# Two transformer blocks on one core: column sums for two norms, token sums for three, modulation sums in parts, and down units by tile

## The reference

```
mod = silu(c) @ ada_w + ada_b                 # six vectors of 2048: shift, scale, gate, twice
h = modulate(rms_norm(x), shift_a, scale_a)   # norm x0
proj = h @ w_in                               # latents q (512), kv (256), rope key, 8 heads of differential q, k, v
q = rms_norm(q_lat) @ w_uq ; kv = rms_norm(kv_lat) @ w_ukv      # norms q and kv
y = concat(mla attention, rms_norm(differential attention)) @ w_o
x = x + gate_a * rms_norm(y)                  # norm y1
h = modulate(rms_norm(x), shift_f, scale_f)   # norm x1
y = (gelu(conv(h @ w_up)_gate) * conv(h @ w_up)_value) @ w_down
x = x + gate_f * rms_norm(y)                  # norm y2
```

## Time and profile before

| | |
|---|---|
| median of three runs | 1850.67 us |
| profiled execution | 1848.06 us, its span 1846.0 us |
| mean granted TensorE clock | 0.966 of full speed |
| PE busy | 1760.6 us (95% of the span) |
| DVE busy | 1245.1 us (67%) |
| ACT busy | 905.2 us (49%) |
| POOL busy | 103.0 us (6%) |
| moved by DMA | 377.15 MB, mean 204 GB/s |

### The profile page before, as it was taken

One profiled execution on the slowest core, in us unless ns is written; L12 is line 12 of the kernel. 1 busy time (PEld: TensorE's weight loads), 2 busy tenths in 40 slices (PEclk: granted clock), 3 DMA queues, 4 the chain that ended last, 5 costly groups with the idle time before them and its releaser, 6 DMA issues.

```text
span 1846.0 us, 33909 instructions
## 1 busy us (share of the span) xinstructions
PE 1760.6 (95%) x14140; PEld 1717.7 (93%) x14140; DVE 1245.1 (67%) x1784; ACT 905.2 (49%) x1490; POOL 103.0 (6%) x61
## 2 busy tenths in 40 slices
PE   4799999999999999999999999999799999999997
PEld 3799889999999999999999999999799999998897
DVE  7996899696667667667667656655564565655653
ACT  8454445454555445445445445434544654555543
POOL 0002331123200000000000000000000000000000
PEclk9899999899979999999999999999799999999998
DMA  9798788587817656656666655544145433653331
GB/s 377 300 406 301 243 269 289 188 284 265 307 55 245 222 195 229 218 197 229 216 201 227 217 187 183 183 161 160 58 161 175 145 126 134 232 196 117 110 116 46
DMA packets 103255, 377.15 MB, mean 204 GB/s; under 512 B 11584, under 2 KB 11968, under 8 KB 102976
## 3 DMA queue, kind: packets, MB, share of 16 engines
q1 hardware_dynamic: 103104, 374.99, 58.6%
HBM read 372.85 MB, written 2.10 MB: 203 GB/s over the span
## 4 chain that ended last, share of the span: by engine, by line
PE 86%; DVE 8%; issue 3%; DMA 1%; ACT 1%; DVEq 0%; SPq 0%; ACTq 0%
PE ps L580 25%; PE ps L581 24%; PE ps L582 24%; DVE ada_acc L1495 3%; PE ps L689 2%; PE ps L631 2%; PE ps L611 1%; DMA raw<-in_ada 1%; PE ps L723 1%; PE ps L708 1%; PE ps L731 1%; DVE w_lo L1480 1%; DVE probs L1626 1%; PE ps L673 1%; DVE stats L1600 1%
## 5 line engine op out<-in xcount | busy, mean ns | idle before, releaser
L580 PE MATMUL ps<-h_hi,w_hi 128*128 128x256 f32 x3264 | 946.1, 290 | 12.1 <-DVE h_lo L1562 6.2
L581 PE MATMUL ps<-h_lo,w_hi 128*128 128x256 f32 x3264 | 929.6, 285 | 0.0
L582 PE MATMUL ps<-h_hi,w_lo 128*128 128x256 f32 x3264 | 929.1, 285 | 0.0
L1480 DVE TENSOR_TENSOR w_lo<-raw,w_hi 128x1024 fp32r<-128x1024 f32 x481 | 587.9, 1224 | 312.7 <-ACT w_hi L1084 310.0
L1084 ACT ACTIVATE w_hi<-raw 128x1024 fp32r<-128x1024 f32 x512 | 539.8, 1056 | 427.9 <-PE ps L582 402.0
L580 PEld LDWEIGHTS ps<-h_hi,w_hi 128*128 128x128 f32 x3264 | 632.4, 194 | 18.2 <-issue 15.1
L581 PEld LDWEIGHTS ps<-h_lo,w_hi 128*128 128x128 f32 x3264 | 632.6, 194 | 1.1
L582 PEld LDWEIGHTS ps<-h_hi,w_lo 128*128 128x128 f32 x3264 | 632.3, 194 | 0.0
L1495 DVE SCALAR_TENSOR_TENSOR ada_acc<-raw,c_act,ada_acc 128x1024 f32<-128x1024 f32 x180 | 236.0, 1323 | 4.4 <-DMA raw<-in_ada 0.8
L580 PE MATMUL ps<-g_hi,w_hi 128*128 128x256 f32 x704 | 199.4, 283 | 3.7 <-DVE g_lo L1862 3.7
L582 PE MATMUL ps<-g_hi,w_lo 128*128 128x256 f32 x704 | 198.6, 282 | 0.0
(11 more groups left out here) (220 smaller groups left out, 1347.0 us busy)
## 6 DMA issues: line engine op xcount, KB each, us to landing
raw<-in_weights SPq DMA_DIRECT2D x512, 512.0 KB, 4.2
raw<-in_ada SPq DMA_DIRECT2D x192, 512.0 KB, 4.9
x<-in_x SPq DMA_DIRECT2D x1, 2048.0 KB, 13.9
out_y<-x SPq DMA_DIRECT2D x3, 512.0 KB, 2.8
consts<-in_consts SPq DMA_DIRECT2D x1, 798.0 KB, 7.9
out_y<-x SPq DMA_DIRECT2D x2, 256.0 KB, 3.1
params<-in_params SPq DMA_DIRECT2D x1, 504.0 KB, 6.4
probs<-in_pos_q SPq DMA_DIRECT2D x1, 128.0 KB, 2.0
```

What stands on the lines that cost most here:

```text
L580: nc.tensor.matmul(out, wh, hi[:, k, :], start=start, stop=False)
L581: nc.tensor.matmul(out, wh, lo[:, k, :], start=False, stop=False)
L582: last = nc.tensor.matmul(out, wl, hi[:, k, :], start=False, stop=stop)
L1480: V.tensor_tensor(w_lo[:, h % W_SLOTS, :], raw[:, raw_slot("w", h), :], w_hi[:, h % W_SLOTS, :].bitcast(F32), ALU.subtract).then_inc(lo_dv ...
```

## The change

- The sums of x1 and x2 go by `mean_square` (256 moving columns). ACT's root reads the sums in PSUM and does the division and epsilon itself; DVE inverts 256 columns; there is no widening, and `modulate` reads `rstd` in SBUF.
- The sums of x0, q and kv go by `token_sums`; their root and inverse have two columns, and a widening puts them in PSUM, from where the scales read them. kv's scale moves from unit 12 to unit 10.
- Sum 4 is issued in four parts behind steps 2 to 5, sum 5 in four parts behind units 11 to 14 of w_o's first pass, sum 6 in four parts behind units 11 to 14 of its second pass, sum 7 in eight parts behind the last eight down units of the fifth group. The waits stand before the first part. `PLAN` brings the ada blocks of sum 6 forward, from one behind each of 15 units to 15 behind the first 11.
- In the last feed-forward group the first four down units run tile by tile, each tile as it is ready.
- A root of one column (`root_table`) is taken by ACT ahead of the loops for y1, y2 and x3, outputs that nothing reads. For y1 the low part of one half moves from before the mean to between mean and inverse.

```diff
@@ -168,3 +168,3 @@
         + [2, 2, 2, 1, 2, 2, 2, 1, 2, 2, 1, 1, 1, 2, 1, 1]
-        + [1] * 15 + [0])
+        + [2, 1, 2, 1, 2, 1, 1, 1, 2, 1, 1] + [0] * 5)
 PLAN_FIRST = [64 + sum(PLAN[:n]) for n in range(len(PLAN) + 1)]
...
@@ -518,5 +519,9 @@
         SCALED = dict(y1=0, y2=len(CHUNKS))
-        TOKEN = dict(y1=0, x1=1, y2=2, x2=3, x3=4)
-        WIDE_BANK = dict(y1=5, x1=3, y2=2, x2=3, x3=2)
+        TOKEN = dict(x0=0, q=1, kv=2, y1=3, y2=4, x3=5)
+        TOKEN_TILES = dict(x0=KT, q=4, kv=2, y1=KT, y2=KT, x3=KT)
+        TOKEN_COLUMN = dict(x0=0, q=0, kv=8, y1=0, y2=0, x3=0)
+        WIDE_BANK = dict(x0=7, q=6, kv=6, y1=5, y2=2, x3=2)
+        WIDE_COLUMN = dict(x0=0, q=0, kv=S, y1=0, y2=0, x3=0)
         NORM = dict(x0=0, q=1, kv=2, y1=3, x1=4, y2=5, x2=6, x3=7)
+        FEATURES = dict(x0=D, q=512, kv=256, y1=D, y2=D, x3=D)
         HN = dict(x0=0, x1=16, x2=32)
...
@@ -603,12 +608,15 @@
-            def mod_sum(n):
+            def mod_sum(n, part=0, parts=1):
                 v, first, end = SUMS[n]
-                pe.wait_ge(ada_used, 1 + max(ADA_AT[v, b, KT - 1] for b in range(first // SLAB, end // SLAB)))
-                if n >= 2:
-                    pe.wait_ge(mod_ready, n - 1)
-                for f in range(first, end):
+                if part == 0:
+                    pe.wait_ge(ada_used, 1 + max(ADA_AT[v, b, KT - 1] for b in range(first // SLAB, end // SLAB)))
+                    if n >= 2:
+                        pe.wait_ge(mod_ready, n - 1)
+                size = (end - first) // parts
+                for f in range(first + size * part, first + size * part + size):
                     last = nc.tensor.matmul(ps[:, SCORE + n % 2, f:f + 1], ada_acc[:, v % 2, f * P:f * P + P],
                                             mean_mat[:, 0:1], start=True, stop=True)
-                last.then_inc(mod_summed, 1)
+                if part == parts - 1:
+                    last.then_inc(mod_summed, 1)
...
@@ -797,5 +806,7 @@
             pe.wait_ge(bias_ready, 6)
-            mean_square("x0", KT)
+            for k in range(KT):
+                token_sums("x0", k)
             mod_sum(0)
             pe.wait_ge(bias_ready, 8)
+            widen("x0")
             mod_sum(1)
@@ -817,7 +828,12 @@
                 if j == 6:
-                    mean_square("q", 4)
+                    for k in range(4):
+                        token_sums("q", k)
                 elif j == 8:
-                    mean_square("kv", 2)
+                    pe.wait_ge(mean_ready, TOKEN["q"] + 1)
+                    for k in range(2):
+                        token_sums("kv", k)
+                    widen("q")
+                elif j == 10:
+                    widen("kv")
                 elif j == 9:
-                    pe.wait_ge(mean_ready, NORM["q"] + 1)
                     pe.wait_ge(unit_evac, U_IN_B + KR + 1)
@@ -847,5 +863,7 @@
                     diff(14 + g)
-                elif g == 5:
+                if g == 2:
                     pe.wait_ge(exps_done, M_MLA)
-                    mod_sum(4)
+                if g in (2, 3, 4, 5):
+                    mod_sum(4, g - 2, 4)
+                if g == 5:
                     sub_sums()
@@ -873,5 +891,6 @@
                     step(m_maps, j - 1)
-                if j == 13:
+                if j == 11:
                     pe.wait_ge(exps_done, M_B)
-                    mod_sum(5)
+                if 11 <= j < 15:
+                    mod_sum(5, j - 11, 4)
             for j in range(KT):
@@ -880,8 +899,7 @@
                     token_sums("y1", j - 1)
+                if 11 <= j < 15:
+                    mod_sum(6, j - 11, 4)
             token_sums("y1", KT - 1)
             widen("y1")
-            mod_sum(6)
-            for k in range(KT):
-                token_sums("x1", k)
-            widen("x1")
+            mean_square("x1", KT)
@@ -911,8 +929,17 @@
                     unit(u + j, range(FF_GROUP), g_hi, g_lo)
-            mod_sum(7)
+                    if g == FF_FULL - 1 and j >= 8:
+                        mod_sum(7, j - 8, 8)
             for j in range(2 * FF_LAST):
                 unit(U_FFL + j, range(KT), h_hi, h_lo)
-            pe.wait_ge(g_lo_done, FF_TILES)
+            u = U_FFL + 2 * FF_LAST
+            for t in range(FF_LAST):
+                pe.wait_ge(g_lo_done, FF_GROUP * FF_FULL + t + 1)
+                for j in range(4):
+                    if t == 0:
+                        bank_free(u + j)
+                        pe.wait_ge(*lo_done(half_of(u + j)))
+                    product(UNIT_FIRST[u + j] + t, ps[:, BANK[u + j], 0:S], t, g_hi, g_lo, t == 0, t == FF_LAST - 1)
             for j in range(KT):
-                unit(U_FFL + 2 * FF_LAST + j, range(FF_LAST), g_hi, g_lo)
+                if j >= 4:
+                    unit(u + j, range(FF_LAST), g_hi, g_lo)
                 if j >= 4:
@@ -922,5 +949,3 @@
             widen("y2")
-            for k in range(KT):
-                token_sums("x2", k)
-            widen("x2")
+            mean_square("x2", KT)
             pe.wait_ge(consts_cast, 2)
@@ -1103,9 +1128,15 @@
                 n = NORM[stage]
-                act.wait_ge(mean_ready, n + 1)
-                nc.scalar.activation(rstd[:, n % 2, :], rstd[:, n % 2, :], ACT.Sqrt).then_inc(root_ready, 1)
+                act.wait_ge(sq_used, SQ[stage] + KT)
+                nc.scalar.activation(rstd[:, n % 2, :], ps[:, NORM_BANK[stage], 0:S], ACT.Sqrt, bias=eps_col[:, 0:1],
+                                     scale=1.0 / D).then_inc(root_ready, 1)
             def token_root(stage):
-                act.wait_ge(mean_ready, NORM[stage] + 1)
+                act.wait_ge(mean_ready, TOKEN[stage] + 1)
                 r = token_r[:, TOKEN[stage], :]
-                nc.scalar.activation(r, r, ACT.Sqrt, bias=eps_col[:, 0:1], scale=1.0 / D).then_inc(root_ready, 1)
+                nc.scalar.activation(r, r, ACT.Sqrt, bias=eps_col[:, 0:1], scale=1.0 / FEATURES[stage]
+                                     ).then_inc(root_ready, 1)
+
+            def root_table():
+
+                nc.scalar.activation(table_out[:, :], eps_col[:, :], ACT.Sqrt)
@@ -1218,3 +1249,3 @@
             hi(1)
-            root("x0")
+            token_root("x0")
             act.wait_ge(mod_ready, 2)
@@ -1245,5 +1276,5 @@
                     squares("kv", 2, lambda k: proj1[:, KVLAT + k, :], (unit_evac, lambda k: U_IN_B + KVLAT + k + 1))
-                    root("q")
+                    token_root("q")
                 elif j == 9:
-                    root("kv")
+                    token_root("kv")
                 elif j == 14:
@@ -1297,2 +1328,3 @@
                     step1(m_maps, j - 1, take_mla)
+            root_table()
             for j in range(KT):
@@ -1308,3 +1340,3 @@
             squares("x1", KT, lambda k: x[:, k, :], (x_ready, lambda k: XN["y1"] + k + 1))
-            token_root("x1")
+            root("x1")
             act.wait_ge(mod_ready, N_SUMS[SH_F])
@@ -1357,3 +1390,3 @@
             squares("x2", KT, lambda k: x[:, k, :], (x_ready, lambda k: XN["y2"] + k + 1))
-            token_root("x2")
+            root("x2")
             h_high("x2")
@@ -1513,9 +1547,2 @@
-            def mean(stage, tiles, n_features):
-
-                n = NORM[stage]
-                dve.wait_ge(sq_used, SQ[stage] + tiles)
-                V.tensor_scalar(rstd[:, n % 2, :], ps[:, NORM_BANK[stage], 0:S], 1.0 / n_features, EPS, ALU.mult,
-                                ALU.add).then_inc(mean_ready, 1)
-
             def invert(stage):
@@ -1527,6 +1554,10 @@
-                dve.wait_ge(sq_used, SQ[stage] + KT)
+                at, tiles = TOKEN_COLUMN[stage], TOKEN_TILES[stage]
+                dve.wait_ge(sq_used, SQ[stage] + tiles)
                 V.reduce_sum(token_r[:, TOKEN[stage], :],
-                             ps[:, NORM_BANK[stage], 0:2 * KT].rearrange("p (a k) -> p a k", a=2), AX
+                             ps[:, NORM_BANK[stage], at:at + 2 * tiles].rearrange("p (a k) -> p a k", a=2), AX
                              ).then_inc(mean_ready, 1)
+
+            def token_invert(stage):
+
                 dve.wait_ge(root_ready, NORM[stage] + 1)
...
@@ -1725,3 +1756,3 @@
                 if i == 29:
-                    mean("x0", KT, D)
+                    token_mean("x0")
                     dve.wait_ge(lam_exp, 1)
@@ -1731,3 +1762,3 @@
                     mod_out(0)
-            invert("x0")
+                    token_invert("x0")
             modulate("x0", lambda k: scale_cols[:, 0, k:k + 1], SH_A, 0, SLAB, 4, 1)
@@ -1749,3 +1780,3 @@
                         V.scalar_tensor_tensor(out=normal_in(HN["x0"] + k), in0=x[:, k, :],
-                                               scalar=scale_cols[:, 0, k:k + 1], in1=rstd[:, NORM["x0"] % 2, :],
+                                               scalar=scale_cols[:, 0, k:k + 1], in1=wide("x0"),
```

(31 more changed lines are left out.)

16 lines of the change are left out of this document (9 added, 7 removed).

## The result

| | before | after |
|---|---|---|
| median | 1851.22 us (4 runs, 1847.46 to 1852.44) | 1832.82 us (4 runs, 1831.11 to 1832.85) |
| profiled execution, its span | 1848.06, 1846.0 us | 1832.85, 1831.0 us |
| mean granted TensorE clock | 0.966 | 0.983 |
| DVE on ada blocks (180 of them) | 236.0 us | 246.2 us |

The ratio after to before is 0.9902, 95% interval 0.9885 to 0.9919: the changed kernel is 18.4 us faster by the medians and 15.2 by the two profiled executions. The forecast was 1827 in a range of 1816 to 1838. The sum of the prediction was -22.3, so some 4 us are missing by the medians and 7 by the profiles, where before's own execution was 3 us quicker than its median.

A forecast was written before the change was run, and what follows sets the result against it. PE, holding 86% of the last-ending chain, was taken to bound the kernel, its clock mattering most. Terms sum to -22.3 from 1848.06, giving 1825.8 us; with the median 2.6 above the profiled run, it forecast 1827, range 1816 to 1838.

The forecast's parts named there:

- the forecast's own case: Whole kernel: 1819 to 1833 us from the bounds of the latent norms, sum 4 and the clock's warm-up; chance 0.69.
- x1, -6.1: Norm x1: without sum 6 ahead, wide sums warm the clock and end 6.5 us earlier, chain behind +0.4; -6.1 us.
- x2, -3.8: Norm x2: wide sums end 4.2 us earlier, with no modulation sum in front, chain behind +0.4; -3.8 us.
- The rival of sums at 1.2 GHz throughout: x1 and x2: the wide sums stay at 1.2 GHz, price 4.2 us in each, 1835 us; chance 0.12.
- q and kv, -5.1: Latent norms: shorter DVE queue cuts PE's wait before the turned values, -3.0 us; scores avoid half clock, -2.1 us.
- Sum 4, -3.0: Subln sums: with sum 4 in parts ahead, they run some 3 us at full pace and end 3.0 us earlier.
- Sum 5, -1.7; sum 7, -1.7: Behind these modulation sums: issued in parts, the clock holds instead of 3.4 us at half rate; 1.7 us saved each.
- down units, -4.0: Last feed-forward group: first four down units, run tile by tile, end 4.8 us earlier, y2 sum waits 0.7; -4.0 us.
- Sum 6 inside w_o, +3.0: w_o's second pass: sum 6's parts cost PE 3.5 us less 0.5 of waiting; DVE has room for ada blocks; +3.0 us.
- x0, +1.6: Norm x0: narrow sums take 13.7 us instead of 9.85, delaying DVE's ada blocks before sum 1; +1.6 us.
- Root tables, -1.5: Norms y2 and x3: root table loaded early while ACT waits for PE, 0.75 us each, nothing at y1; -1.5 us.
- Slower, mixed stretches at 1.2 GHz: w_o and down units with sums in parts: rival, clock falls, 46 us of products take twice as long, 1873; chance 0.04.

The follow-up runs named there:

- e11_before_wide: Kernel before with only the sums of x1 and x2 over 256 moving columns, root and inverse over 256 columns too: 1842.2 us, ratio 0.9956.
- e10_undone: Changed kernel with sums 4, 5 and 7 in one piece at their old places and the last group's first four down units whole: 1837.43 us.
- e1_pad_after: Changed kernel with 96 unused bytes per partition behind eps_col: 1830.03 us, ratio 0.989 to the kernel before.
- e9_best: Changed kernel with 32 unused bytes ahead of x, sum 6 in four parts behind w_o, old ada plan, x0 sums over 256 columns: 1792.51 us.
- e8_x0_wide: Changed kernel with the x0 sums over 256 moving columns again, without widening: 1829.78 us, ratio 0.9886 to the kernel before.
- e7_pad_all: Changed kernel with 32 unused bytes ahead of raw, the first tensor, so weights and moving operands move together: 1831.77 us, ratio 0.9898 to the kernel before.
- e4_pairs: Changed kernel with the ada blocks of w_o's second pass shifted by a unit, two where DVE makes the low part: 1830.95 us.
- e2_pad_x: Changed kernel with 32 unused bytes per partition ahead of x: 1799.81 us, ratio 0.9736 to the kernel before.

## Why the prediction was right, and where it was short

The direction, the range and the likeliest case held: 1832.8 against 1827 in 1816 to 1838, at the upper edge of the 1819 to 1833 of the forecast's own case. Part of that is luck. Two costs that it had not seen came to some 7 us, and the kernel came out so near only because smaller terms gave about 2 us more than forecast. The number 1827 also does not follow from its sum: 1825.8 and the 2.6 by which the median lay above the profiled execution are 1828.4, and in the changed kernel the two agree (1832.82 and 1832.85). Point by point:

- *x1, -6.1* and *x2, -3.8*: -6.1 and -4.4 measured. The steps hold as well: the sums took 10.18 us (9.55 forecast) but started 0.5 us sooner behind the widening, and the chain behind them took 4.2 (4.3). e11_before_wide shows the wide sums alone. The rival of sums at 1.2 GHz throughout fell with the rows of line 626.
- *q and kv, -5.1*: PE's wait of 4.4 us is gone (0.45 us with kv's widening stand in its place, from 199.07 to 199.52), and the clock is 1.00 from 195 to 207 us where the earlier trace rows had 0.50 from 204 on. The stage up to the first turned values gave -3.8, and from there to the first subln sum it is 132.3 us instead of 133.9, -1.7: together -5.5. No run undid this part alone.
- *Sum 4, -3.0*: 0.0 (e10_undone). From the first subln sum to the widening are 15.3 us instead of 17.0, but e10_undone has the same 15.4 with sum 4 whole. The step that failed is "with less narrow work ahead they run some 3 us at full pace": it took the moment at which the clock falls for a thing that the length of the narrow work fixes. 24 records of the subln sums took 3.46 us here and 3.86 behind a whole sum, against 5.16 before; in e1_pad_after and e9_best, behind the same parts, 2.82 and 4.01.
- *Sum 5, -1.7; sum 7, -1.7; down units, -4.0*: sum 7 and the down units gave 5.6 between them, 5.8 when undone; sum 5's low clock of some 1.7 us is absent after and back in e10_undone.
- *Sum 6 inside w_o, +3.0*: this is the mis-sized term. It measured 6.9 in its stage (156.5 less 149.5 us), less 1.1 for the shorter stage behind. PE's side was costed rightly, 0.76 us in each of four units; the failing sentence is that the four ada blocks "lie on DVE, which has room there, since GpSimd makes every second low part". GpSimd's low parts are not only relief: an ada block that starts beside one takes 3.1 to 3.4 us. The bound of +5 was put down to late loads, and that was the wrong cause as well: no engine waited for a load there.
- *x0, +1.6*: +0.6 in the profile, 1.4 by the first product of e8_x0_wide.
- *Root tables, -1.5*: -1.6.
- *Slower, mixed stretches at 1.2 GHz*: did not happen; PEclk is 1.00 in the parts of sums 5 and 7.
- *Not in the list at all*: two words more in `token_r` and a new tensor shifted `g_hi` to a distance of 0 from the weights (modulo 256 bytes), 0.64 us in each full group's down stage and 0.3 in the last group's, +3.5 in the profile. The prediction took a moved tensor for nothing and gave neither a term nor a bound for it.

So of the 7 us that the profile misses, 3.9 are sum 6, 3.5 the addresses and 1.4 the subln sums (-3.0 forecast, -1.6 there, though not through sum 4), and some 2 come back from x0, x2, q and kv.

## What to carry to other kernels

Before work is moved between engines, look in the trace at how long an instruction takes when it starts beside one of GpSimd, not only at how much room its queue has: here 1.27 us became 3.4, and a unit's readout stood behind it. A gap in which PE waits for another engine's chain is a better place for small sums than a stretch that PE paces. And when every matmul of a kernel reads the same two kinds of tensors, try their distance: 32 bytes of padding gave more here than the whole change.

## What the runs showed of the hardware that was not expected

- The time of a 128x128 by 256 fp32r matmul with its weight load depends on where its two operands lie to each other: 0.1200 us at distances 0 and 96 modulo 256 bytes, 0.1183 at 224, 0.1178 at 64, 0.1167 at 32. When weights and moving operand move together it stays at 0.1200 (e7_pad_all), so the distance counts and not the address. At 0, 32 and 64 h and g, which lie some 82,000 bytes apart, agree. Other distances were not tried, nor was the modulus; why it is so stays open.
- An ada block of DVE (two SBUF inputs) that starts beside a running low part of GpSimd stands until that has ended: 3.08 to 3.42 us instead of 1.27, in every pair of the changed kernel's second w_o pass and every single block started beside GpSimd in e4_pairs. Each of them ended 1.08 us behind the low part.
- The same 32 wide sums of x1 took 10.18, 10.18, 8.75, 8.66 and 8.71 us in the changed kernel, e4_pairs, e1_pad_after, e2_pad_x and e9_best: the clock rises at another point of them, from the same low clock at their start.
